# Moving the split activation tiles from 32 to 112 bytes past a multiple of 128 in a four-layer fp32 model kernel

## The reference

```
first block:   x += fox_mixer(rms_norm(x));  x += sq_relu_mlp(rms_norm(x), w_up, w_down)      (d_ff 4096)
               k, k_rope, v = mla_shared_kv(x);  x += mla_mixer(rms_norm(x));  x += sq_relu_mlp(...)
second block:  x += gla_mixer(rmsnorm(x));   x += conv_ffn(rmsnorm(x), w_up, conv_w, w_down)  (d_ff 2816)
               x += short_conv_mixer(...);   x += conv_ffn(...)
sq_relu_mlp(h, w_up, w_down) = square(relu(h @ w_up)) @ w_down
```

## Time and profile before

| | |
|---|---|
| median of 3 runs | 1177.66 us (1177.17 to 1177.95) |
| profiled execution | 1179.46 us, of which its span is 1177.6 us |
| PE busy | 1161.7 us (99%) |
| PEld busy | 1136.7 us (97%) |
| DVE, ACT, POOL busy | 866.8, 651.6, 267.0 us |
| HBM read | 201.57 MB |

### The profile page before, as it was taken

How to read it: one execution, slowest core, us unless ns; L and a number is a source line. 1 busy time by engine, 2 the same in 40 slices (tenths; PEclk the granted TensorE clock), 3 DMA queues, 4 the chain that set the end, 5 groups by cost and what they waited for, 6 DMA issues and landing times.

```text
span 1177.6 us, 26235 instructions
## 1 busy us (share of the span) xinstructions
PE 1161.7 (99%) x9706; PEld 1136.7 (97%) x9706; DVE 866.8 (74%) x1387; ACT 651.6 (55%) x1075; POOL 267.0 (23%) x256
## 2 busy tenths in 40 slices
PE   9999999999999999999999999999999999999997
PEld 8998999999987999999999999999999999999997
DVE  6866777656696877755577488898768778999854
ACT  6656556544446555644555556666555455666543
POOL 0001400012230600011200263444321025444421
PEclk9999999999999999999999999999999999999999
DMA  9643665555652566465454255554656555565451
GB/s 304 194 143 108 191 194 185 180 185 171 161 162 82 179 187 200 158 205 180 142 186 157 95 168 171 189 182 147 196 188 208 190 180 179 180 201 181 146 197 59
DMA packets 213136, 203.51 MB, mean 173 GB/s; under 512 B 11840, under 2 KB 212800, under 8 KB 213072
## 3 DMA queue, kind: packets, MB, share of 16 engines
q1 hardware_dynamic: 212928, 202.44, 53.5%
q10 hardware_dynamic: 144, 0.20, 0.1%
HBM read 201.57 MB, written 1.05 MB: 172 GB/s over the span
## 4 chain that ended last, share of the span: by engine, by line
PE 94%; DVE 3%; ACT 1%; issue 1%; DMA 0%; POOL 0%; DVEq 0%; ACTq 0%; SPq 0%; POOLq 0%
PE gemm L712 28%; PE gemm L713 28%; PE gemm L714 28%; PE gemm L723 2%; PE gemm L724 1%; PE gemm L725 1%; DVE w_lo L1609 1%; PE score L905 1%; PE score L1024 1%; DMA x<-in_xT 0%; ACT w_hi L1237 0%; PE misc L750 0%; PE score L1027 0%; ACT act_a L1255 0%; PE score L1127 0%
## 5 line engine op out<-in xcount | busy, mean ns | idle before, releaser
L1609 DVE TENSOR_TENSOR w_lo<-w_raw,w_hi 128x1024 fp32r<-128x1024 f32 (+2 forms) x404 | 481.4, 1196 | 159.2 <-ACT w_hi L1237 157.4
L1237 ACT CAST w_hi<-w_raw 128x1024 fp32r<-128x1024 f32 (+2 forms) x404 | 401.5, 999 | 162.1 <-PE gemm L714 154.4
L712 PE MATMUL gemm<-act_a,w_hi 128*128 128x256 f32 (+1 forms) x1704 | 479.5, 281 | 1.4 <-DVE w_lo L1609 1.0
L713 PE MATMUL gemm<-act_a,w_hi 128*128 128x256 f32 (+1 forms) x1704 | 476.4, 280 | 0.0
L714 PE MATMUL gemm<-act_a,w_lo 128*128 128x256 f32 (+1 forms) x1704 | 475.0, 279 | 0.0
L712 PEld LDWEIGHTS gemm<-act_a,w_hi 128*128 128x128 f32 (+1 forms) x1704 | 318.7, 187 | 6.0 <-DVE w_lo L1609 2.3
L713 PEld LDWEIGHTS gemm<-act_a,w_hi 128*128 128x128 f32 (+1 forms) x1704 | 318.8, 187 | 0.4
L714 PEld LDWEIGHTS gemm<-act_a,w_lo 128*128 128x128 f32 (+1 forms) x1704 | 318.8, 187 | 0.4
L712 PE MATMUL gemm<-hid,w_hi 128*128 128x256 f32 x864 | 241.8, 280 | 0.0
L713 PE MATMUL gemm<-hid,w_hi 128*128 128x256 f32 x864 | 241.3, 279 | 0.0
L714 PE MATMUL gemm<-hid,w_lo 128*128 128x256 f32 x864 | 240.9, 279 | 0.0
(11 more groups left out here) (273 smaller groups left out, 1391.2 us busy)
## 6 DMA issues: line engine op xcount, KB each, us to landing
w_raw<-in_ffn_w_up SPq DMA_DIRECT2D x76, 1024.0 KB, 5.2
w_raw<-in_ffn_w_down SPq DMA_DIRECT2D x32, 1024.0 KB, 4.9
w_raw<-in_gla_w_in SPq DMA_DIRECT2D x12, 1024.0 KB, 5.3
w_raw<-in_ffn_w_down SPq DMA_DIRECT2D x16, 768.0 KB, 4.3
w_raw<-in_sc_w_in SPq DMA_DIRECT2D x12, 1024.0 KB, 5.2
w_raw<-in_fox_w_in SPq DMA_DIRECT2D x10, 1024.0 KB, 6.8
w_raw<-in_ffn_w_down SPq DMA_DIRECT2D x16, 640.0 KB, 3.9
w_raw<-in_fox_w_out SPq DMA_DIRECT2D x4, 1024.0 KB, 4.8
```

The source lines that it names most:

```text
L712: nc.tensor.matmul(ps, wh[:, k, cols], act[:, k0 + k, 0, :], start=start and k == 0, stop=False)
L713: nc.tensor.matmul(ps, wh[:, k, cols], act[:, k0 + k, 1, :], start=False, stop=False)
L1237: nc.scalar.copy(split_half(w_hi, nc_, nj), raw_half(nc_, nj)).then_inc(w_hi_ready, 1)
L1609: nc.vector.tensor_tensor(split_half(w_lo, nc_, nj), raw_half(nc_, nj), split_half(w_hi, nc_, nj).bitcast(F32), ALU.subtract).then_inc(w_l ...
```

## The change

`split_tiles` gets an argument `past`. It moves the next free address to `past` rounded down to 32, past a multiple of 128, allocates the tensor `past % 32` bytes larger, and hands out a view that leaves these first bytes out. `act_a`, `act_b` and `hid` then start at 112 bytes past a multiple of 128 (a tensor at 96 and 16 bytes left out), `m_act` at 104 (8 bytes left out). No instruction is added, removed or moved on any engine; the shapes stay.

```
-        def split_tiles(name, n):
+        def split_tiles(name, n, past):
             start = used[0]
-            used[0] += (32 - start) % 128
-            return sb(name, [P, n, 2, T], F32R)
+            used[0] += (past // 32 * 32 - start) % 128
+            skip = past % 32 // 4
+            return sb(name, [P, skip + n * 2 * T], F32R)[:, skip:].rearrange("p (n s t) -> p n s t", s=2, t=T)
...
-        act_a = split_tiles("act_a", KD)
-        act_b = split_tiles("act_b", KD)
+        act_a = split_tiles("act_a", KD, past=112)
+        act_b = split_tiles("act_b", KD, past=112)
...
-        hid = split_tiles("hid", DFF // P)
+        hid = split_tiles("hid", DFF // P, past=112)
...
-        m_act = split_tiles("m_act", 5)
+        m_act = split_tiles("m_act", 5, past=104)
```

## The result

| | before | after |
|---|---|---|
| median | 1177.41 us (1176.42 to 1177.95, 4 runs) | 1163.50 us (1163.33 to 1165.22, 4 runs) |
| profiled execution | 1179.46 us, span 1177.6 | 1163.33 us, span 1161.5 |
| ratio | | 0.9864 (95% interval 0.9842 to 0.9887) |

A forecast was written before the change was run, and what follows sets the result against it. TensorE, busy 99%, was taken to bound the kernel by its matmul spacing. All stages at 116.7 ns gave -3.5 us, all other terms 0: 1177.7 less 3.5 is 1174.2 us, range 1163 to 1186 (8 in 10).

The forecast's parts named there:

- the upper level: TensorE's slower matmul spacing, 117.8 ns against 116.7, on 3120 matmuls in some stages; leaving it was worth -3.5 us.
- TensorE's distance is the time: Kernel time is 9084 matmuls times the distance between starts; one nanosecond is 9.1 us, or 0.8%.
- Two levels at an unchanged position, dealt at the start of a stage: Matmul stages hold 116.7 or 117.8 ns at the same addresses, presumably by the phase in which a stage begins.
- So 0 and 32 cost the same: Moving reads 0 or 32 bytes past a 128-byte multiple were claimed to cost alike: 116.4 and 116.7 ns per 256 columns.
- the 24 extra clocks: The 10.0 ns by which 116.7 ns per matmul exceeds 256 columns at one per clock, 106.7 ns.
- The term for `act_a`, `act_b` and `hid`: Moving reads of the three large tensors at 112 bytes: all stages taken at 116.7 ns, -3.5 us.
- `m_act` and the token stages at 0: `m_act` at 104, 1 us either way, and stationary `act_a` in token stages, 0.4 us at 1 ns each: both put at 0.
- What the profile after would show: Expected signs: U0, CU0 with CD0, SI with SO at 116.7 ns, durations 280 ns; wrong if under 116.6 or at 120.
- The larger gain: Rival, chance 0.13: a better offset avoids collisions in TensorE's stream, giving 1164 us or less (-14 to -35 us).
- The lost phase: Rival: the new offset puts all stages on 117.8 ns, +6.7 us, about 1184; chance 0.18 for all or most.
- the much slower case: Rival, chance 0.10: the half step costs every matmul an extra step, 120.0 ns, +27 us, 1205 us.
- The cacheline rule: SBUF reads cost by 16-byte lines crossed: large tensors cost nothing new, only `m_act` touches 65 lines; sum 0.

The follow-up runs named there:

- The swept kernels: No model, only feature_block matmuls: moving tensor or weights started 0 to 252 bytes past a multiple of 256, in 4-byte steps; moving at 112 gave 113.3 ns.

## Why the prediction was wrong

The sign was right and TensorE's stream was the right place to look; the size and its reason were not. -3.5 us were forecast by way of the upper level, -13.9 were measured by way of a lower one, and 1163.5 lies at the low end of the range. That it came out faster at all was luck: with the same `past` and `act_a` 128 bytes further on it is 1180.5. By its own steps:

- **TensorE's distance is the time.** Right. The table by tensor adds up to 16.3 us of the 16.1 between the spans, with nothing on any writer (a lo tile of `hid` takes 420 ns in both traces, one of `act_a` 761 and 762). The waits on the way of the weights are 156.4 and 154.3 us against 157.4 and 154.4.
- **Two levels at an unchanged position, dealt at the start of a stage.** Right as far as two traces go: the second of the kernel before has U0, U1 and SI with SO on other levels. But the new position didn't deal between these two: it had levels of its own, 113.3 on `act_a` and 117.15 on `hid`.
- **"So 0 and 32 cost the same, and the 24 extra clocks don't come from the distance to a 128-byte line."** This is the step that failed. From two pairs of addresses with one cost I took it that no start changes the lower level. Both rows hold a distance of 32 bytes between moving and stationary operand, one way and the other, and the second is of 512 columns, which have a map of their own (226.7 to 234.6 ns). The swept kernels show 113.3 to 124.4 ns over 64 positions. The trace of the kernel before spoke against the step already. In stage GV the weights move at 0 with `act_a` stationary at 32, in 256 columns; between these two rows lie 69 distances, 8.17 / 69 = 118.4 ns, neither of the two levels (118.21 over all such distances):

```profile
617.51 0.28 PE L724 MATMUL gemm<-w_hi,act_a 128*128 128x256 f32 x1
...
625.68 0.28 PE L724 MATMUL gemm<-w_hi,act_a 128*128 128x256 f32 x1
```

- **The term for `act_a`, `act_b` and `hid`.** -3.5 us was the price of the upper level alone, 1.11 ns for 3120 matmuls. Measured between the two profiled executions, it is -18.3 on `act_a` (3.6 ns for 5053) and +0.8 on the two others. I had priced the three together, by their place within 128 bytes, though the diff leaves open where they fall within 256. The period of 256 was nowhere in the working.
- **`m_act` and the token stages at 0.** Small as said: +0.5 and +0.7 us against bounds of 1 and 0.4. The second bound was too narrow: 1.8 ns for each, not 1.
- **What the profile after would show.** U0, CU0 and SI at 116.7 was wrong (113.4), as were durations of 280 ns throughout (277 on `act_a`); "a distance under 116.6 in any long stage (then the 24 clocks were to be had)" is what came. Eight of the 24 were.
- **The rivals.** The larger gain, given 0.13, named 113.3 ns as one step of 8 clocks fewer in each matmul, which is exactly the level found, and 1164 for a step in every third. The total agrees with that number by luck, for another reason: a full step on one tensor out of three, which holds 5112 of the 9084 matmuls, and the median of the runs moved 2 us less than the profiled executions. My argument against it, that the moving operand at 0 cost the same, was the failed step again. The lost phase and the much slower case did not come, but both exist: 120.0 ns is the commonest level of the swept list, and the kernel with everything 16 bytes on took 1195 us.
- **The cacheline rule.** The Trainium skill ("SBUF — State Buffer", "Door 1: The DMA port swizzle") has reads cost by the 16-byte lines crossed. In part the runs agree: with `m_act` at 104 its distance went from 117.2 to 120.8 ns, and positions 4 and 8 bytes past a multiple of 16 mean 121.3 and 120.1 ns against 117.8 on one. But 12 bytes past means 118.3, and among multiples of 16 the distance spreads from 113.3 to 120.1, so the rule doesn't give the cost here, and its sum of 0 was wrong by 14 us.

What stays open: why a matmul has 113.3 ns at best where 256 columns at one per clock would be 106.7, what in the reading of the two operands gives the steps of 8 clocks and the period of 256 bytes, and what chooses among the levels of a pair. The runs show the map, not the mechanism. `w_hi` and `w_lo` stood alike within 256 bytes in every run, as did hi and lo of a tile; other arrangements weren't tried.

## What to carry to other kernels

Where TensorE streams without a break, read the distance between starts per tensor to 0.1 ns; if it is above columns over clock, the start addresses of moving and stationary operand within 256 bytes are worth 6% between good and bad. A small kernel that sweeps the positions on an idle chip gives one reading of each in one run (26 of 32 came out the same a second time); before a position is used, it has to be run in the whole kernel several times, since some pairs have two or three levels (four executions 13.1 us apart) and others showed only one (four within 0.4 us, and again 113.3 to 113.4 ns in every long stage with both 32 bytes on). Here weights at 128 and moving tensors at 240 past a multiple of 256 make 1150.9 us of 1178.3.

## What the hardware showed that was not expected

- fp32r matmuls of 256 columns at a granted clock of 1.00 (2.4 GHz) run at 113.3 to 124.4 ns with nothing changed but the pair of addresses; 13 of 128 pairs in steps of 16 bytes reach the lowest in one reading.
- Moving both operands by 128 bytes changes nothing (117.14 and 117.13 ns on `act_a`, 113.41 on `hid` and 113.39); moving both by 16 does (113.59 to 118.64 on `act_a`).
- The same pair can stream at two or three steady levels, which then hold for up to 1500 matmuls and more (CU0 with CD0, 117.8): 116.7 and 117.8 at distance 32, 113.3 and 117.8 at 192, 116.7, 118.3 and 120.0 with weights at 16 past a multiple of 32 at distance 112.
- 512 moving columns at a distance of 0 take 226.7 ns, where 256 columns at that distance take 120.0 each.
